# Half-depth weight chunks for the recurrent layer's whole input projection, with forget gate and query transposed afterwards

## The reference, cut to what matters

```python
def rmsnorm(x, g):
    y = xf * lax.rsqrt(jnp.mean(xf * xf, axis=-1, keepdims=True) + EPS)
    return (y * g.astype(jnp.float32)).astype(x.dtype)

def hgrn2_mixer(h, norm_g, w_in, lb, out_g, w_out):
    xn = rmsnorm(h, norm_g)
    q, fr, i, g = jnp.split(xn @ w_in, 4, axis=-1)
    q = jax.nn.silu(q.astype(jnp.float32))
    f = lb + (1.0 - lb) * jax.nn.sigmoid(fr.astype(jnp.float32))
    k = 1.0 - f
    logf = jnp.log(f)
    ...                      # recurrence over chunks, o = inter + intra
    o = rmsnorm(o, out_g) * jax.nn.silu(g)
    return o @ w_out
```

## Time and profile before

| | us |
|---|---|
| median of 3 runs | 1640.22 |
| lowest and highest | 1638.34, 1641.25 |
| time of the profiled execution | 1638.91 |
| its span, first to last instruction | 1636.8 |
| busy in the span: PE, DVE, ACT, POOL | 1134.2, 1122.1, 272.6, 1054.2 |
| first gather issued at | 126.5 |

### The profile page before, as it was taken

The page is one execution under the profiler, slowest core; times in us unless marked ns, Lnnn a source line. Parts: engine busy times, 40 slices in busy tenths (PEclk is TensorE's granted clock), DMA queues, the critical chain, the costliest instruction groups (busy, mean ns, idle before and its releaser), DMA issues.

```text
span 1636.8 us, 16492 instructions
## 1 busy us (share of the span) xinstructions
PE 1134.2 (69%) x5152; PEld 688.3 (42%) x5152; DVE 1122.1 (69%) x2947; ACT 272.6 (17%) x806; POOL 1054.2 (64%) x1030
## 2 busy tenths in 40 slices
PE   7988777786787458865578667786668755545556
PEld 7976454354464135533335334343326521111122
DVE  2659887675675886965566688685657796767552
ACT  2222112121113101111111201111211311111110
POOL 0007776775765677667765677667776577777772
PEclk9999888898898788977799778997889977777778
DMA  9878999999999999999999999999999999999997
GB/s 353 318 320 302 379 387 410 411 412 410 412 411 412 409 407 406 412 411 409 409 413 412 410 389 400 413 412 409 410 411 411 357 411 409 410 409 409 409 409 304
DMA packets 164245, 647.16 MB, mean 395 GB/s; under 512 B 18624, under 2 KB 18880, under 8 KB 151616
## 3 DMA queue, kind: packets, MB, share of 16 engines
q0 software_dynamic: 147456, 536.94, 82.8%
q1 hardware_dynamic: 16704, 109.17, 16.5%
HBM read 644.99 MB, written 1.05 MB: 395 GB/s over the span
## 4 chain that ended last, share of the span: by engine, by line
DMA 38%; POOL 21%; issue 16%; DVE 12%; PE 11%; ACT 1%; POOLq 0%; DVEq 0%; ACTq 0%; PEldq 0%
DMA v_ring<-in_v,idx_all 18%; DMA u_ring<-in_u,idx_all 17%; POOL u_ring L451 10%; POOL v_ring L451 10%; PE acc L1536 8%; DVE u_ring L927 4%; DMA arena<-in_v,idx_all 3%; DVE w_ring L927 1%; DVE xn L509 1%; POOL arena L451 1%; PE bank L1294 1%; PE bank L1272 1%; DVE arena L509 1%; PE bank L1298 1%; POOL w_ring L451 1%
## 5 line engine op out<-in xcount | busy, mean ns | idle before, releaser
L1536 PE MATMUL acc<-v_ring,diag 128*64 128x512 f32 x1536 | 481.8, 705 | 258.4 <-ACT diag L1194 207.6
L451 POOL DMA_INDIRECT u_ring<-in_u,idx_all x448 | 456.8, 1020 | 276.7 <-issue 129.6
L451 POOL DMA_INDIRECT v_ring<-in_v,idx_all x448 | 473.5, 1057 | 237.0 <-PE acc L1536 137.4
L927 DVE SCALAR_TENSOR_TENSOR u_ring<-u_ring,xrep 128x1024 f32<-128x1024 f32 x384 | 463.1, 1226 | 208.2 <-DMA u_ring<-in_u,idx_all 197.0
L1536 PEld LDWEIGHTS acc<-v_ring,diag 128*64 128x64 f32 x1536 | 196.7, 159 | 522.5 <-issue 261.1
L1536 PE MATMUL acc<-arena,gains 128*64 128x512 f32 x256 | 85.2, 731 | 75.2 <-DMA arena<-in_v,idx_all 74.8
L1536 PE MATMUL acc<-v_ring,gains 128*64 128x512 f32 x256 | 85.2, 705 | 71.7 <-DMA v_ring<-in_v,idx_all 71.1
L1181 ACT ACTIVATE ez<-zi 128x8 f32<-128x8 f32 x64 | 13.4, 209 | 575.2 <-DVEq L937 572.5
L1298 PE MATMUL bank<-w_ring,xT 128*128 128x256 f32 x448 | 103.8, 393 | 4.9 <-ACTq L981 4.9
L1294 PEld LDWEIGHTS bank<-xT,w_ring 128*128 128x128 f32 x896 | 103.2, 196 | 6.6 <-issue 5.7
L1294 PE MATMUL bank<-xT,w_ring 128*128 128x128 f32 x896 | 104.8, 280 | 0.5 <-ACTq L981 0.5
(11 more groups left out here) (176 smaller groups left out, 1246.0 us busy)
## 6 DMA issues: line engine op xcount, KB each, us to landing
w_ring<-in_wall SPq DMA_DIRECT2D x86, 1024.0 KB, 8.5
u_ring<-in_u,idx_all POOLq DMA_INDIRECT x448, 16.7
v_ring<-in_v,idx_all POOLq DMA_INDIRECT x448, 16.8
u_ring<-in_wall SPq DMA_DIRECT2D x4, 1024.0 KB, 10.0
v_ring<-in_wall SPq DMA_DIRECT2D x3, 1024.0 KB, 9.3
arena<-in_wall SPq DMA_DIRECT2D x3, 1024.0 KB, 10.7
gains<-in_gains SPq DMA_DIRECT2D x5, 512.0 KB, 13.4
kept<-in_wall SPq DMA_DIRECT2D x2, 1024.0 KB, 12.5
```

The costliest lines, as they stand in the source:

```text
L451: nc.gpsimd.indirect_dma_start(out=ring[:, r, :], out_offset=None, in_=table, in_offset=bass.IndirectOffsetOnAxis(ap=idx_all[:, at:at + 1] ...
L927: V.scalar_tensor_tensor(out=ring[:, r, :], in0=ring[:, r, :], scalar=1.0, in1=token_rows(phase)[r % PACK], op0=ALU.mult, op1=ALU.mult, ac ...
L1536: ins = M(acc[half(r % PACK), s], diagonal((first + n) * RING + r)[0], ring[:, r, s], start=False, stop=last and q + PACK == RING)
```

## The change

All chunks of `w_in`, `w_out`, `w_kv` and `w_q` (rows `W_IN` to `W_O`) now hold half the depth (4 blocks) of 512 output columns. The stored weights stay as they are: a load takes one half of each row of two neighbouring chunks, so each partition's 8 KB come in two runs of 4 KB. `project_chunk` does 4 matmuls of 512 columns instead of 8 of 256, and forget gate and query, before 16 of 128, use it too. Their results have tokens on partitions, so 16 transposes a tile (4 groups of 4) bring them into channel layout: `forget(c, turn)` into `scp`, `query(c, turn)` into `tr`. VectorE reads the forget gate from `scp`, ScalarE takes the query from `tr` with two instructions a half. VectorE multiplies `xn` by the gain alone and gives it to TensorE; after that it computes the token's factor, copies it and its half into `hs`, and raises `norm_ready`. ScalarE applies it as `scale` in its copies. `lower_bound` follows that. Value's third chunk now comes ahead of `scores(0)`. `PIECES` of layer 0 has two pieces of 512. The diff, cut to its core:

```diff
-PIECES = (((0, 512, 2, 0), (512, 256, 1, 512), (768, 256, 1, 0)), ...
+PIECES = (((0, 512, 2, 0), (512, 512, 2, 512)), ...
@@ load @@
+                if WIDE_FIRST <= row < WIDE_END:
+                    pair, s = row - row % 2, slice(row % 2 * CHUNK // 2, (row % 2 + 1) * CHUNK // 2)
+                    src = wall_d[pair:pair + 2, :, s].rearrange("c p m -> p c m")
+                    to = lambda a: a.rearrange("p (c m) -> p c m", c=2)
@@ VectorE hgrn @@
-                token_rsqrt(t)
                 if t == 0:
                     dve.wait_ge(consts_in, 16 * EARLY)
-                    ... (xn = h * factor * gain in halves, lower_bound; tile 1: at once)
+                for c in range(2):
+                    s = slice(c * 512, (c + 1) * 512)
+                    link(tt(xn[:, s], h[:, t, s], gains[:, GAIN_HG, s], ALU.mult))
+                    dve.sem_inc(to_transpose, 1)
+                token_rsqrt(t, ke)
+                tick(V.tensor_copy(hs[:, 0:1], rs[:, 0:1]))
+                link(V.tensor_scalar(hs[:, 1:2], rs[:, 0:1], 0.5, None, ALU.mult))
+                dve.sem_inc(norm_ready, 1)
+                if t == 0:
+                    lower_bound()
@@ ScalarE hgrn @@
+                act.wait_ge(norm_ready, t + 1)
+                take_half(0, tanh_of(ke))
+                yield
+                take_half(1, tanh_of(ke))
+                take_half(0, (qe, ACT.Copy, whole))
+                yield
+                give(eT, raw, ACT.Ln)
+                give(eT, eT, ACT.Exp)
+                take_half(1, (qe, ACT.Copy, whole))
+                take_query(0)
+                take_half(0, (vi, ACT.Copy, whole))
+                take_query(1)
@@ TensorE @@
+                w = next_chunk().rearrange("p (c k n) -> p k c n", c=2, k=KT_D // 2)
+                for k in range(KT_D // 2):
+                    at = c * KT_D // 2 + k
+                    ins = M(out[:, :].rearrange("p (c n) -> p c n", c=2), xT[:, at, :], w[:, k, :, :], ...)
+                project_wide(1)
+                forget(0, turn)
+                project_wide(1)
+                forget(1, turn + 1)
+                yield
+                project_wide(1)
+                query(0, turn + 2)
+                project_wide(1)
+                query(1, turn + 3)
+                yield
+                value = take_turn()
+                project_chunk(value, 0)
+                pe.wait_ge(pair_read, count.pairs)
                 scores(0)
                 scores(1)
-                value = take_turn()
-                project_chunk(value, 0)
```

More of the change, by code:

```diff
@@ L215, in build @@
         hr = sb("hr", [P, 1])
+        hs = sb("hs", [P, 2])
         warm = sb("warm", [P, 1])
@@ L605, in hgrn @@
                     link(V.tensor_copy(lmask[:, :, :].rearrange("p l t -> p (l t)"), on))
-                wait_next(projected)
-                for n in range(HG_HEADS):
-                    c = slice(n * P, (n + 1) * P)
-                    (link if n == HG_HEADS - 1 else tick)(
-                        V.tensor_scalar(raw[:, c], raw[:, c], lb_b[:, n:n + 1], lb_a[:, n:n + 1], ALU.mult, ALU.add))
+                for c in range(FORGET):
+                    from_pe()
+                    count.pairs += 1
+                    for n in range(4 * c, 4 * c + 4):
+                        s = slice(n * P, (n + 1) * P)
+                        (link if n % 4 == 3 else tick)(
+                            V.tensor_scalar(raw[:, s], scp[:, s], lb_b[:, n:n + 1], lb_a[:, n:n + 1], ALU.mult, ALU.add))
+                    pair_is_read()
                 ask()
@@ L1057, in hgrn @@
                 count.chunks += 4
-                count.banks += 3
+                count.banks += 2
                 yield
@@ L1278, in lent_read, with project_wide, project_across @@
                 pe.sem_inc(lent_free, 1)
-            def project(turns, across, by_half=False):
-                pe.wait_ge(transposes_read, count.transposes - (1 if by_half else 0))
+            def project_wide(turns):
+                pe.wait_ge(transposes_read, count.transposes)
+                for _ in range(turns):
+                    out = take_turn()
+                    for c in range(2):
+                        project_chunk(out, c)
+            def project_across(turns):
+                pe.wait_ge(transposes_read, count.transposes)
                 for _ in range(turns):
@@ L1319, in scores, with query, forget @@
                     ins.then_inc(pair_full, 1)
-                if t == 0:
-                    for c in range(2):
-                        transpose_part(width(xn)[4 * c:4 * c + 4], c, c * 512)
-                else:
-                    transpose_new(width(xn))
-                project(1, True, t == 0)
+                def query(c, turn):
+                    pe.wait_ge(bank_read, turn)
+                    pe.wait_ge(transposes_read, count.transposes - c)
+                    if c == 0:
+                        pe.wait_ge(pair_read, count.pairs - FORGET)
+                    for n in range(4 * c, 4 * c + 4):
+                        s = slice(n * P, (n + 1) * P)
+                        ins = nc.tensor.transpose(tr[:, s], qe[:, s], ident[:, :])
+                    ins.then_inc(transposed, 1)
+                    count.transposes += 1
+                def forget(c, turn):
+                    pe.wait_ge(bank_read, turn)
+                    if c == 0:
+                        pe.wait_ge(pair_read, count.pairs)
+                    for n in range(4 * c, 4 * c + 4):
+                        s = slice(n * P, (n + 1) * P)
+                        ins = nc.tensor.transpose(scp[:, s], ke[:, s], ident[:, :])
+                    ins.then_inc(pair_full, 1)
+                    count.pairs += 1
+                for c in range(2):
+                    transpose_part(width(xn)[4 * c:4 * c + 4], c, c * 512)
+                out = take_turn()
+                for c in range(2):
+                    pe.wait_ge(transposes_read, count.transposes - 1 + c)
+                    project_chunk(out, c)
+                turn = count.banks
                 yield
-                project(2, True)
+                project_wide(1)
+                forget(0, turn)
+                project_wide(1)
+                forget(1, turn + 1)
                 yield
-                project(1, True)
-                project(1, False)
+                project_wide(1)
+                query(0, turn + 2)
+                project_wide(1)
+                query(1, turn + 3)
                 yield
+                value = take_turn()
+                project_chunk(value, 0)
+                pe.wait_ge(pair_read, count.pairs)
                 scores(0)
                 scores(1)
-                value = take_turn()
-                project_chunk(value, 0)
                 yield
@@ L1386, in hgrn @@
                 out = take_turn()
-                w = next_chunk().rearrange("p (k n) -> p k n", k=KT_D)
-                for k in range(KT_D):
-                    if k % 4 == 0:
-                        pe.wait_ge(transposes_read, count.transposes - 1 + k // 4)
-                    ins = M(out[:, 0:256], xT[:, k, :], w[:, k, :], start=k == 0, stop=k == KT_D - 1)
-                ins.then_inc(w_used, 1)
-                project_chunk(out, 1)
-                for _ in range(2):
-                    project_chunk(take_turn(), 0)
+                for c in range(2):
+                    pe.wait_ge(transposes_read, count.transposes - 1 + c)
+                    project_chunk(out, c)
+                project_wide(1)
                 yield
```

98 lines of the change are left out of this document (42 added, 56 removed).

## The result

The changed kernel took 1654.7 us, the median of four runs (1654.22 to 1656.86), and the kernel before 1640.09 in the same comparison (four runs, 1638.34 to 1641.25). The ratio is 1.0087 with a 95% interval of 1.0075 to 1.0099: slower by 14.6 us, where +7.8 was predicted. The direction was right, the size was outside the range, and outside the wider range of 1641 to 1653 too. The profiled execution took 1654.22 with a span of 1652.0, 15.2 above the span before.

What follows compares the result with a forecast made beforehand. TensorE was taken to pace the prologue, DMA and GpSimd's feeding the rest. Prologue +5.8, loads +2.5 and tile 1 -0.5 gave +7.8 on 1638.91, or 1646.7, forecast as a median of 1648.0 us; range 1644 to 1651, 8-in-10 1641 to 1653.

Steps and rivals of the forecast that it cites:

- What bounds the kernel: Whole kernel: TensorE paces the prologue, DMA the rest; a later first gather pushes everything behind it one for one.
- What they wait for is done: the banks are read during the turn in between.: Added transposes in the prologue: they wait for nothing, so only their own work is priced, +1.8 us.
- `query(1)` ahead of `scores(0)`: Last transpose group in the prologue: fits by 0.1 or 0.2 us; if not, some tenths are lost.
- The clock: TensorE's slow stretch at the start: costs about 2.4 us as before, only moved with the first matmul; 0 in the sum.
- Everything at its full price: Rival: loads cost 4.1, the clock falls again for 0.9, some tenths for `query(1)`; 1651.6 us, chance 0.20.
- The start: Start of tile 0: ScalarE's copies queue behind the exponential awaiting `lower_bound`; first matmul at 12.77 against 11.02, +1.75 us.
- Wider matmuls and added transposes: Prologue on TensorE: 512-column forget and query chunks -0.7 us (bounds 0 and -1.3), four transpose groups +1.8 us.
- The moved chunk: Value's third chunk no longer covers VectorE's operands, so TensorE waits at `scores(2)`: +1.9 us (1.5 to 2.2), paid once.
- The last piece: Prologue end, ahead of `head(0)`: last 256 columns become 512, lengthening VectorE's steps, transposes and copy; +1.0 us (0.5 to 1.2).
- The loads: Behind the first gather: 37 chunks in 4 KB runs compete with gathers for DMA; +2.5 us (0 to 4.1).
- Tile 1 beside the gather: Tile 1's first turn ends sooner, but GpSimd waits for next to nothing there; -0.5 us (-1.5 to +1.0).
- the first rival: Smooth issues win: tile 1's earlier start ends GpSimd's stretched gather issues, up to 16 us back; 1632 us, chance 0.10.

Runs made afterwards that it cites:

- changed, again: The changed kernel with nothing altered, timed and profiled a second time; 1655.84 us, ratio 1.0089 to the kernel before.
- value turn free of query: Changed kernel with value's first turn no longer waiting for ScalarE's reading of query(0)'s transposes; 1650.9 us, ratio 1.0063 to the kernel before.
- query inside the turn: Changed kernel with query(1)'s transposes between the two chunks of value's first turn, third chunk back between scores(1) and scores(2); 1647.43 us, ratio 1.0042.
- changed, 8 KB: Changed kernel with weights laid out so a half-depth chunk is one 8 KB run per partition; 1653.18 us, beside the changed kernel's 1655.84.
- four repairs: Changed kernel with value turn not waiting for query copies, lower_bound ahead of factor, later chunks one place earlier, 8 KB runs; 1646.17 us, ratio 1.0031.
- query inside, three repairs: Changed kernel, query(1)'s transposes inside value's first turn, third chunk moved back, lower_bound ahead of factor, last piece in halves, 8 KB runs; 1642.62 us, ratio 1.0006.
- before, one wait (timed): Kernel before, with TensorE made to wait ahead of value's first turn until ScalarE has read the previous turn's bank; 1645.73 us, ratio 1.003.

## Why the prediction failed, step by step

The times on the chips where the kernel before took 1640 to 1641 us follow, to about 1 us, from two numbers, the first gather (of the profiled execution) and the size of the runs:

| kernel | first gather against 126.51 | time against the kernel before | run size |
|---|---|---|---|
| changed | +13.7 | +14.6 | 4 KB |
| changed, again | +13.8 | +14.7 | 4 KB |
| value turn free of query | +9.0 | +10.2 | 4 KB |
| query inside the turn | +5.3 | +6.5 | 4 KB |
| changed, 8 KB | +14.1 | +12.0 | 8 KB |
| four repairs | +5.0 | +5.0 | 8 KB |
| query inside, three repairs | +2.8 | +1.6 | 8 KB |
| before, one wait (timed) | +6.3 | +4.8 | 8 KB |

The column of times less that of the gathers is 0.9, 0.9, 1.2 and 1.2 with runs of 4 KB, and -2.1, 0.0, -1.2 and -1.5 with runs of 8 KB: 1.1 and -1.2 on average. The kernel before with one wait has nothing changed behind its first gather and still stands at -1.5, so some -1.2 is the zero of this column: 126.51 comes from a single execution, which was itself 1.3 faster than the median. What counts is the 2.3 between the two groups.

**What bounds the kernel.** Right: the prologue is paid about one for one.

**The failed step: "What they wait for is done: the banks are read during the turn in between."** That sentence priced the added transposes' work and looked only at what the transposes wait for. It did not look at what the next turn waits for once they are issued. `project_wide` waits for every transpose read so far, and the query's are read behind ScalarE's exponential, which VectorE releases late. That is 2.80 us, and 1.76 of slow clock behind it, in a term that stood at 0 (its own stated risk, `query(1)` ahead of `scores(0)`, did not come: nothing waits at 59.64). Taking the wait away gave 4.4 us in time.

**The clock, the second term that failed.** In the sum it stood at 0, and the rival *Everything at its full price* gave it 0.9; that rival's 1651.6 was the nearest of the four, and still 3.1 short. In the profiled execution it cost 1.76 behind the missed wait, 3.42 behind the forecast wait at `scores(2)`, and about 0.9 around the product into `acc`: 6.1 in all, the largest item. It differs from execution to execution. Behind the wait of 1.17 at `scores(2)` it fell in four profiles of the changed kernel and its variants and stayed up in three; behind the wait of 2.8 at the value turn it fell in three and stayed up in two; behind the 2.99 in the kernel before it did each once. Where these waits are absent, it never fell at these two places: not in seven profiles at the value turn, nor in seven at `scores(2)`. In these profiles a fall there came only behind a stop. The product into `acc` was slow in all eleven profiles of the changed kernel and its variants, and in one of three of the kernel before and its variant. What decides between a fall and none stays open, and so does whether the change itself makes the fall at `acc` likelier.

**The start.** Right in mechanism: +2.16, where 1.75 was forecast; the first matmul came at 13.18 and not at 12.77. The two multiplications took 1.69 with their gap, not 1.4 (VectorE's squares begin at 8.00, the multiplications at 6.31), and the constants landed 0.1 later; every other term of that chain was within 0.03.

**Wider matmuls and added transposes.** -0.7 and +1.8 were forecast. By ScalarE's readings the columns gave 4 x 0.35 = 1.4 back, a little past the far bound, and four groups at 0.50 took 2.0. With the 0.2 that the start of the clock gave back, the two rows of the table come to +0.4, where +1.1 was forecast.

**The moved chunk.** A wait at `scores(2)` came as forecast, released by VectorE: 1.3 from start to start, under the lower bound of 1.5, where 1.9 was expected. VectorE started the operands 3.44 us behind TensorE's first product of `scores(0)`, and before it was 3.87 (52.92 less the first product at 49.05). But "this is paid once" left out the clock behind it.

**The last piece.** +0.87, forecast +1.0.

**The loads.** +2.5 forecast; 2.7 in time between the two kernels that differ in nothing else, and 2.3 by the averages under the table. By price it would be 0.10 us a chunk, 3.7 for 37; where the rest went isn't shown. The estimate from the overhead a packet in the Trainium skill (DMA: Bandwidth & Descriptors, Why small descriptors are slow) was 0.03 us a chunk and 1.0 in all; the measured price is over three times that, and it decides.

**Tile 1 beside the gather.** From the first gather to the end the changed kernel took 1511.8 us and the kernel before 1510.3. With the loads at +2.5 this stage gave about -1.0. But single profiles differ by 2 us. On the quiet chips the other three profiles with runs of 4 KB took 1513.8, 1514.0 and 1514.2 from there, the three with runs of 8 KB 1511.2, 1509.7 and 1512.2, and the kernel before with its one wait 1509.6 and 1510.3. The averages are 1513.5, 1511.0 and, with the kernel before, 1510.1: 2.4 for the runs of 4 KB, and about +1.0 for tile 1, where -0.5 was forecast and +1.0 was the bound. Between -1.0 and +1.0 a finer answer isn't to be had. GpSimd's gathers from 150 to 330 us show no release of the kind that the first rival needed; its mean issue of a u row is 1037 ns, not under 1000:

```profile
L460 POOL DMA_INDIRECT v_ring<-in_v,idx_all x64 | 71.5, 1118 | 23.6 <-issue 18.0 <-PE acc L1588 5.6
L460 POOL DMA_INDIRECT u_ring<-in_u,idx_all x58 | 60.2, 1037 | 25.7 <-issue 17.1 <-DVE u_ring L941 8.6
```

**The sum.** Forecast for the prologue +5.8. The forecast terms came out at 2.16 + 0.43 + 1.27 + 0.87 = 4.7. The missed wait is 2.8, the clock 6.1, together 13.6 of 13.7. Behind the first gather it was +1.5 in this profile and +3.4 on the average of four, forecast +2.0. The terms are those of one execution, and the clock's share changes with the execution; the second profile of the changed kernel had the same two falls and the same size of loss (first gather +13.8).

## What to carry to other kernels

When a step is put between two others, ask not only what it waits for but what the next instruction's wait will now include: a semaphore counted as "all so far" takes in everything that was added. Where a dense engine gets a new stop of one to three us, put what a fall of the clock cost here, 1.7 to 3.4 us, into the range, and leave 0 in it too. And a new step that needs a round trip through another engine is best placed in the middle of a long piece of work that doesn't need it; that alone, without any change of the arithmetic, took back 8 of 14.6 us.

## What the runs showed of the hardware

The granted clock can fall behind a stop as short as 1.17 us in an otherwise full stretch (in 4 profiles of 7; in 0 of 7 without the stop), and need not fall behind one of 2.99: one program, run twice, had 7.17 and 8.86 us for the same turn behind the same wait. The Trainium skill (TensorE: Matmul & The Clock Gate, Part 1: The HAM clock gate) says that the number of slow matmuls at a kernel's start varies from run to run. The profiles agree for the start (the first 32 matmuls of 512 columns took 15.57 us in one and 16.87 in another, with the same wait ahead of them), and the same holds in the middle.

A run of 4 KB instead of 8 KB costs 2.51 against 2.41 us a MB while all DMA engines are full, and direct loads and gathers of the same run size cost the same (2.51 both).
